# First feed-forward products of seven rounds: weights standing, high and low x moving side by side, hidden layer not transposed

## The chip, the cores and the metric

The kernel runs on one core of a Trainium2 chip. The metric is the device time of one execution in microseconds (us); lower is better. Engines: TensorE (PE in the rows; its weight loads are PEld), VectorE (DVE), ScalarE (ACT), GpSimd (POOL) and the sync engine (SP), whose queue issues the loads.

## What is computed

The reference is two transformer blocks one after the other, on 256 tokens of width 2048, in float32. The change touches the feed-forward part of the first block:

```
def sq_relu_mlp(h, w1, w2):
    return jnp.square(jax.nn.relu(h @ w1)) @ w2
x = x + gm * sq_relu_mlp(modulate(x, norm_mlp_w[l], sm, cm), w_ff1[l], w_ff2[l])
```

w_ff1 is 2048 x 8192, w_ff2 is 8192 x 2048. `gm`, `sm` and `cm` are conditions, products of a vector with columns of w_mod.

## The kernel before

Every large product is made from split operands: a float32 weight tile is loaded (`raw`, four slots of 1 MB), ScalarE rounds it to fp32r (`whi`, line 591), VectorE takes the difference (`wlo`, line 1085), each in two halves, and TensorE adds three products: high x times high weight, low x times high weight, high x times low weight. A **unit** is one 1 MB load: 512 rows of the weight by 512 columns, `whi` and `wlo` hold two units each. The semaphore `units_used` counts halves that TensorE is done with; ScalarE may round unit u's half once TensorE is done with the same half of unit u-2. The loads are issued by SP in one fixed order (line 394), load n once load n-4 has been used up.

`multiply` (line 1867) makes the products of a unit: for each pair of k-tiles and each of the two blocks of 128 tokens it loads x as the standing operand (128 x 128) and moves 512 weight columns through, 24 matmuls in all (line 1887). The result is in rows of tokens.

The feed-forward phase (`mlp`) is eight **rounds** of 16 units, e = 0 to 7 (`quarter` in each engine's program). In a round, units 0 to 7 are the first product for 1024 hidden columns, in two groups of four units, each into two PSUM banks. ScalarE takes a group with relu into `hid` (line 857), VectorE squares it (line 1528). The second product needs the hidden layer with its columns on the partitions, so TensorE transposes it (`turn_rows`, line 1968) in 8 pairs of 128-column blocks per token block, that is 16 transposes a round, in runs of 4, 4 and 8; ScalarE rounds each run of four out of PSUM into `hhi` (line 609) and VectorE takes the difference into `hlo` (line 1106). Units 8 to 15 are the second product, four groups of two units, each added into `yacc` (line 1565).

Round 0 begins with its own order (`first_columns`), in which the transposes of the normed x are spread. In rounds 0 to 3 four more loads a round, slices of w_mod, stand in the same four slots behind units 4, 6, 11 and 13 (`CONDITIONS_MLP`), and VectorE sums each with a column of the condition vector (`sum_rows`, lines 1255 and 1257); such a slot is released by `cond_summed`. In round 7 VectorE also adds four finished conditions (`add_condition`, line 1408), which wait for TensorE's sums (line 2153), and TensorE transposes rows for the next phase.

Elsewhere two places have weights standing and x moving, 256 columns at a time: the z gates of both attention phases (`multiply_gate`, line 2308) and the narrow unit of gate columns (line 2478), whose load has rows of 512 B (line 459).

Of the kernel before, what the change touches and what calls it, by code (L numbers as in the profile page):

```python
# [51 lines left out]
          ("mlp", 128, 48), ("a_in", 20, 5), ("a_z", 16, 4), ("a_out", 16, 4), ("b_att", 29, 8), ("b_z", 16, 4),  # L52
# [41 lines left out]
for _u in range(UNITS):  # L94
# [7 lines left out]
          ("a", 8), ("b", 8)]  # L102
BUILD = {}
# [34 lines left out]

def plus(base, step, i):

    return base if i is None else base + step * i


def dit_kernel(nc, a, out):
# [9 lines left out]
    xhi = sb("xhi", [P, KT, L], F32R)  # L154
    xlo = sb("xlo", [P, KT, L], F32R)
# [76 lines left out]
    hid = v3(rows[:, 0:2048], W1)  # L232
# [144 lines left out]
    def _(sp):  # L377
        count = {"load": 0, "plain": 0, "mod": 0, "sum": 0}

        def load(kind, src, narrow=False):  # L380
# [12 lines left out]
            to = raw[:, n % 4].rearrange("p k (c n) -> p (k c) n", n=P) if narrow else raw[:, n % 4]  # L393
            sp.dma_start(to, src.rearrange("(k p) n -> p k n", p=P)).then_inc(raw_in[n % 4], 16)
# [12 lines left out]
        def load_unit(src, narrow=False):  # L407
            u = count["plain"]
            load("plain", src, narrow)
# [49 lines left out]
        load_unit(a["b_w_in"][:, D + 6 * KVG * HD:D + 6 * KVG * HD + P], narrow=True)  # L459
# [114 lines left out]
    def _(act):  # L574
# [279 lines left out]
        def quarter(e, u0, b0, loads=16):  # L854
            def relu(n):
                group_done(u0 + 4 * n + 3, e, 16)
                act.activation(hid[:, :, n * NW:(n + 1) * NW], banks(n), ACT.Relu).then_inc(acc_freed, 1)

            def hidden(g):
                build(b0 + g, 2 * g, hhi, i=e, per=4)  # L860

            split(u0 + 3, 3, e, 16, loads)
            relu(0)
            split(u0 + 6, 2, e, 16, loads)
            hidden(0)
            split(u0 + 8, 1, e, 16, loads)
            hidden(1)
            split(u0 + 9, 1, e, 16, loads)
            relu(1)
            hidden(2)  # L870
            hidden(3)
            for n in range(4):
# [21 lines left out]
        with act.Fori(0, 4) as e:  # L894
            quarter(e, UNIT["mlp"], BUILD["hidden"], loads=20)
# [177 lines left out]
    def _(dve):  # L1073
# [443 lines left out]
        def quarter(e, u0, g0, b0, s0, last=False, conditions=False):  # L1517
            def split_with_condition(u, k):

                for half in range(2):  # L1520
                    split_halves(2 * u + half, 1, e, 16)
                    if conditions:
                        sum_rows(cond_sum[:, bass.ds(e * NW, NW)], SUM["mlp"] + k, k, (2 * half, 2 * half + 1), e)

            def square(n):
                dve.wait_ge(acc_freed, plus(g0 + n + 1, 6, e))
# [3 lines left out]
            def hidden(g):  # L1530
                build(b0 + g, 2 * g, hhi, hlo, i=e, per=4)

            split(u0 + 3, 2, e, 16)
            split_with_condition(u0 + 5, 0)
            square(0)
            if last:
                add_condition(4)
                add_condition(5)
            split(u0 + 6, 1, e, 16)
            split_with_condition(u0 + 7, 1)  # L1540
            hidden(0)
            split(u0 + 8, 1, e, 16)
            hidden(1)
            split(u0 + 9, 1, e, 16)
# [3 lines left out]
            if last:  # L1548
                add_condition(6)
                add_condition(7)  # L1550
            for n in range(4):
                if n in (1, 2):
                    split_with_condition(u0 + 10 + 2 * n, n + 1)
# [7 lines left out]
                cols = slice(n * NW, (n + 1) * NW)  # L1561
                part = yacc[:, :, cols]
                if n == 0:
                    dve.wait_ge(zeroed, 1)
                dve.tensor_tensor(part, banks(n), part, ALU.add).then_inc(acc_freed, 1)
                if last:
                    dve.wait_ge(modcol_taken, 1 + CONDITIONS1 + 8)
                    dve.wait_ge(acc_freed, g0 + 2 + n + 1)
# [14 lines left out]
        with dve.Fori(0, 4) as e:  # L1583
            end = looped(12, 4)
            quarter(e, UNIT["mlp"], GROUP["mlp"], BUILD["hidden"], 0, conditions=True)
# [277 lines left out]
    def _(pe):  # L1863
# [29 lines left out]


# [325 lines left out]
        def quarter(e, u0, g0, b0, s0, first=False, last=False):  # L2220
            def hidden(pairs):
                turn_rows(b0, hid, pairs, i=e, per=4,
                          ready=lambda g: pe.wait_ge(squared, plus(s0 + g // 2 + 1, 2, e)))

            if first:
                first_columns()
            else:
                product(u0, 0, 4, built=built("mlp"), i=e, per=16, g_count=g0, g_per=6)

            pe.wait_ge(acc_freed, plus(g0, 6, e))  # L2230
            for k in range(4):
                multiply(u0 + 4 + k, k, 4, 2, i=e, per=16)
                if last and k in (0, 3):
                    for b in (4, 5) if k == 0 else (6, 7):
                        sum_rows(b)
# [3 lines left out]
            pe.wait_ge(acc_freed, plus(g0 + 1, 6, e))  # L2239
            for tiles in ((0, 1, 2), (3,)):  # L2240
                multiply(u0 + 8, 0, 2, 0, 0, hhi, hlo, e, 16, tiles=tiles, rounded=plus(b0 + 2, 4, e) if tiles[0] == 0 else None)
                if tiles[0] == 0:
                    hidden((2, 3))
            multiply(u0 + 9, 1, 2, 0, 0, hhi, hlo, e, 16, rounded=plus(b0 + 4, 4, e))
            for n in range(1, 4):
                pe.wait_ge(acc_freed, plus(g0 + 1 + n, 6, e))
# [368 lines left out]
```

## Time and profile before

| | |
|---|---|
| median of 3 runs | 2292.61 us (2292.25 to 2293.01) |
| profiled execution: time, span | 2292.78 us, 2291.0 us |
| TensorE, busy share of the span | 99% |
| VectorE, ScalarE, GpSimd | 68%, 46%, 3% |
| share of the chain that ended last: TensorE | 95% |
| mean DMA rate | 207 GB/s |

The time of an execution is a little above the span of its trace. Busy time of matmuls is pipelined: two that follow each other overlap in the rows, so the cost of one is read from the distance between two starts. "Idle before" is the time an engine stood before the instructions of a row, with what released it.

### The profile page before, as it was taken

How to read it: one execution, taken by the hardware profiler on the slowest of the kernel's cores; microseconds unless marked ns; L12 is line 12 of the kernel's file. 1: busy time of each engine (PE TensorE's matmuls, PEld its weight loads, DVE VectorE, ACT ScalarE, POOL GpSimd, SP SyncE). 2: the span in 40 equal slices, each digit the busy share in tenths (PEclk: the TensorE clock that was granted, in tenths of full speed). 3: DMA queues.
4: the chain of work that ended last, by engine and by line, in shares of the span. 5: the costliest groups of instructions: out<-in, count | busy, mean ns of one | idle time of the engine just before them, and what ended most of it. 6: DMA issues, size and time to landing. Idle time of an engine off the chain costs nothing.

```text
span 2291.0 us, 30464 instructions
## 1 busy us (share of the span) xinstructions
PE 2258.2 (99%) x11867; PEld 1853.3 (81%) x11867; DVE 1552.7 (68%) x2299; ACT 1064.8 (46%) x1589; POOL 72.4 (3%) x91
## 2 busy tenths in 40 slices
PE   6999999999999999999999999999999999999998
PEld 3777787877888788888888888888988888899977
DVE  2577798777888776676655555764686545578865
ACT  4343234555543644344444443454555454466644
POOL 1000001110000100000000000000000000000000
PEclk8999999999999999999999999999999999999999
DMA  9989884444689677667656555555444576432243
GB/s 369 334 307 316 299 301 160 146 144 152 222 299 322 211 272 242 223 235 248 229 188 196 183 186 185 180 184 184 157 126 141 184 231 211 157 120 93 93 133 125
DMA packets 235011, 474.61 MB, mean 207 GB/s; under 512 B 7784, under 2 KB 10176, under 8 KB 233872
## 3 DMA queue, kind: packets, MB, share of 16 engines
q1 hardware_dynamic: 231280, 460.35, 59.7%
q0 software_dynamic: 3296, 12.53, 1.6%
q8 instruction: 79, 1.29, 0.2%
q14 instruction: 36, 0.29, 0.0%
q10 hardware_dynamic: 320, 0.13, 0.0%
HBM read 470.89 MB, written 2.10 MB: 206 GB/s over the span
## 4 chain that ended last, share of the span: by engine, by line
PE 95%; DVE 2%; DMA 2%; ACT 1%; issue 1%; SPq 0%; POOLq 0%; POOL 0%; DVEq 0%
PE acc L1887 74%; PE acc L2308 8%; PE acc L2350 2%; PE aux L2384 2%; PE turn L2364 2%; PE aux L1920 1%; PE turn L1968 1%; DMA raw<-in_w_o 1%; DVE wlo L1085 1%; DMA arena<-in_x 1%; PE turn L2105 1%; PE acc L2120 1%; PE turn L2263 0%; PE acc L2090 0%; PE aux L2408 0%
## 5 line engine op out<-in xcount | busy, mean ns | idle before, releaser
L1085 DVE TENSOR_TENSOR wlo<-raw,whi 128x1024 fp32r<-128x1024 f32 x674 | 819.9, 1224 | 550.8 <-ACT whi L591 545.3
L591 ACT ACTIVATE whi<-raw 128x1024 fp32r<-128x1024 f32 x674 | 710.7, 1059 | 975.1 <-PE acc L1887 851.3
L1887 PE MATMUL acc<-whi,xhi 128*128 128x512 f32 x1536 | 424.4, 398 | 4.4 <-ACT xhi L673 2.6
L1887 PE MATMUL acc<-whi,xlo 128*128 128x512 f32 x1536 | 413.0, 390 | 0.5 <-DVE xlo L1485 0.5
L1887 PE MATMUL acc<-wlo,xhi 128*128 128x512 f32 x1536 | 412.7, 390 | 0.0
L1887 PEld LDWEIGHTS acc<-whi,xhi 128*128 128x128 f32 x1536 | 281.2, 188 | 85.8 <-issue 24.9
L1887 PEld LDWEIGHTS acc<-whi,xlo 128*128 128x128 f32 x1536 | 288.6, 188 | 62.7 <-DVE xlo L1485 1.0
L1887 PEld LDWEIGHTS acc<-wlo,xhi 128*128 128x128 f32 x1536 | 288.9, 188 | 61.2
L1887 PE MATMUL acc<-whi,hhi 128*128 128x512 f32 x512 | 139.7, 392 | 0.0
L1887 PE MATMUL acc<-whi,hlo 128*128 128x512 f32 x512 | 138.2, 389 | 0.0
L1887 PE MATMUL acc<-wlo,hhi 128*128 128x512 f32 x512 | 138.2, 389 | 0.0
L1887 PEld LDWEIGHTS acc<-whi,hlo 128*128 128x128 f32 x512 | 96.1, 188 | 20.1
L1887 PEld LDWEIGHTS acc<-wlo,hhi 128*128 128x128 f32 x512 | 96.1, 188 | 20.1
L1887 PEld LDWEIGHTS acc<-whi,hhi 128*128 128x128 f32 x512 | 95.3, 188 | 19.5 <-issue 0.5
L1887 PE MATMUL acc<-whi,ghi 128*128 128x512 f32 x384 | 107.0, 397 | 0.5 <-ACT whi L591 0.5
L1887 PE MATMUL acc<-whi,glo 128*128 128x512 f32 x384 | 104.1, 390 | 0.0
L950 ACT ACTIVATE arena<-arena,m 128x128 f32<-128x128 f32 (+3 forms) x192 | 85.1, 445 | 40.8 <-DVE m L1669 40.8
L1887 PE MATMUL acc<-wlo,ghi 128*128 128x512 f32 x384 | 104.0, 389 | 0.0
L1257 DVE SCALAR_TENSOR_TENSOR arena<-raw,cflat,arena 128x512 f32<-128x512 f32 x120 | 90.0, 750 | 3.5
L1257 DVE SCALAR_TENSOR_TENSOR qkv<-raw,cflat,qkv 128x512 f32<-128x512 f32 (+1 forms) x120 | 89.9, 749 | 2.3
L2308 PE MATMUL acc<-xhi,whi 128*128 128x256 f32 x512 | 86.0, 290 | 0.0
L1887 PEld LDWEIGHTS acc<-whi,glo 128*128 128x128 f32 x384 | 72.1, 188 | 15.3
(329 smaller groups left out, 2329.7 us busy)
## 6 DMA issues: line engine op xcount, KB each, us to landing
raw<-in_w_ff SPq DMA_DIRECT2D x128, 1024.0 KB, 5.2
raw<-in_w_mod SPq DMA_DIRECT2D x96, 1024.0 KB, 7.3
raw<-in_w_in SPq DMA_DIRECT2D x64, 1024.0 KB, 5.3
raw<-in_b_w_in SPq DMA_DIRECT2D x45, 1024.0 KB, 5.0
raw<-in_a_w_in SPq DMA_DIRECT2D x36, 1024.0 KB, 5.1
raw<-in_w_o SPq DMA_DIRECT2D x16, 1024.0 KB, 7.1
raw<-in_a_w_out SPq DMA_DIRECT2D x16, 1024.0 KB, 5.2
raw<-in_b_w_out SPq DMA_DIRECT2D x16, 1024.0 KB, 5.0
```

The costliest lines, as they stand in the source:

```text
L591: act.activation(whi[:, k % 2, on], raw[:, n % 4, on], ACT.Copy).then_inc(hi_ready, 1)
L950: ins = act.activation(x, x, ACT.Exp, scale=-1.0, bias=m8[:, q % 2, k:k + 1], accum_out=s8[:, q % 2, k:k + 1])
L1085: dve.tensor_tensor(wlo[:, k % 2, on], raw[:, LOAD_OF_UNIT[k] % 4, on], whi[:, k % 2, on].bitcast(F32), ALU.subtract)\
L1257: ins = dve.scalar_tensor_tensor(total, raw[:, n % 4, kk], x, total, ALU.mult, ALU.add)
L1887: mm = pe.matmul(acc[:, bank0 + t, :], x[:, tile(kt), t * P:(t + 1) * P], w[:, u % 2, kk], start=kt == k_first and x is hi and w is whi, s ...
L1920: mm = pe.matmul(bank[32 * kk:32 * (kk + 1), :], cflat[:, 2 * kt:2 * kt + 32], raw[:, n % 4, kk], start=k == 0, stop=k == 3, tile_position ...
L1968: mm = pe.transpose(turn[:, n % 2, k * L + t * P:k * L + (t + 1) * P], src[:, t, (2 * g + k) * P:(2 * g + k + 1) * P], ident[:, :])
L2105: mm = pe.matmul(turn[:, c, :], slabT[on, t * P:(t + 1) * P], slabT[on, 256:768], start=True, stop=True)
L2308: mm = pe.matmul(acc[:, 2 + c // 2, c % 2 * L:(c % 2 + 1) * L], w[:, c * P:(c + 1) * P], x[:, kt, :], start=kt == 0 and c % 2 == 0 and w i ...
L2350: mm = pe.matmul(acc[:, c, u * keys:(u + 1) * keys], at["qT"][on, g, t, j, :], at["kT"][u][on, g * L:g * L + keys], start=True, stop=True)
L2364: mm = pe.transpose(turn[:, c, o:o + P], prob[:, c, u, k * P:(k + 1) * P], ident[:, :])
L2384: mm = pe.matmul(aux[c * HD:(c + 1) * HD, n % 2, to:to + w], at["v"](g, u, k), pT[:, 512 * c + o:512 * c + o + w], start=i == k == u == 0, ...
```

## The change

In rounds 1 to 7 the first product is made by a new function, `multiply_turned`. Its unit is 1024 rows of w_ff1 by 256 columns (8 k-tiles, two column blocks; the load has rows of 1 KB in place of 2 KB). 128 x 128 blocks of weights are the standing operand. x moves: `xhi` and `xlo` are now the two halves of one tile `x2`, and 512 columns, 256 of high and 256 of low x, go through the high weights into the two halves of a PSUM bank; then 256 columns of high x go through the low weights into the first half. There are four groups of two units. The result has the hidden columns on the partitions. VectorE adds the two halves (`tensor_reduce`), then makes relu and square in one instruction; ScalarE rounds into `hhi` from SBUF, VectorE takes the difference into `hlo`. The transposes of the hidden layer and ScalarE's relu are gone from these rounds. The sums of conditions stand behind the difference of groups 1 and 2 in place of between the halves of units 5 and 7; in round 7 the additions of conditions stand behind groups 1 and 3. Round 0 keeps its form (`first_quarter`). The second product is as before, but for the hidden tiles that its first two units wait for.

```diff
 PHASES = [("front", 32, 48), ("att", 32, 8), ("up", 16, 8), ("wo", 16, 4),
-          ("mlp", 128, 48), ("a_in", 20, 5), ("a_z", 16, 4), ("a_out", 16, 4), ("b_att", 29, 8), ("b_z", 16, 4),
+          ("mlp", 128, 62), ("a_in", 20, 5), ("a_z", 16, 4), ("a_out", 16, 4), ("b_att", 29, 8), ("b_z", 16, 4),
           ("b_out", 16, 4)]
...
 
 BUILDS = [("front", 16), ("mix", 8), ("mlp", 8), ("hidden", 32),
           ("a", 8), ("b", 8)]
+BUILT_TURNED = 28
...
          12: ("turn", "b_ks"), 13: ("norm", 1), 14: ("turn", "b_kw"), 15: ("turn", "b_q2")}
 
 
+def turned_of(g):
...
     wlo = sb("wlo", [P, 2, UK, NW], F32R)
-    xhi = sb("xhi", [P, KT, L], F32R)
-    xlo = sb("xlo", [P, KT, L], F32R)
+    x2 = sb("x2", [P, 2, KT, L], F32R)
+    xhi, xlo = x2[:, 0], x2[:, 1]
+
+    narrow_hi, narrow_lo = (w[:, :, :, :].rearrange("p s k (c n) -> p s (k c) n", n=L) for w in (whi, wlo))
...
-    hid = v3(rows[:, 0:2048], W1)
+    hid, hid4 = v3(rows[:, 0:2048], W1), v3(rows[:, 0:2048], NW)
...
                     sp.wait_ge(cond_summed, before.count("sum"))
-            to = raw[:, n % 4].rearrange("p k (c n) -> p (k c) n", n=P) if narrow else raw[:, n % 4]
...
         for e in range(8):
-            for n in range(2):
-                for k in range(4):
-                    load_unit(a["w_ff1"][k * 512:(k + 1) * 512, e * W1 + n * NW:e * W1 + (n + 1) * NW])
+            if e == 0:
+                column_blocks(a["w_ff1"], 2)
+            else:
+                for n in range(4):
+                    for k in range(2):
+                        load_unit(a["w_ff1"][k * W1:(k + 1) * W1, e * W1 + n * L:e * W1 + (n + 1) * L], width=L)
             for n in range(4):
                 for k in range(2):
...
-            act.wait_ge(turned, plus(g + 1, per, i))
+            act.wait_ge(turned, plus(turned_of(g), per, i))
...
+        def first_quarter():
+            u0, b0 = UNIT["mlp"], BUILD["hidden"]
+
...
+            split(u0 + 10, 9)
+
+        def quarter(e, u0, b0, loads=16):
+            for g in range(4):
+                split(u0 + 3 + 2 * g, 1, e, 16, loads)
+                act.wait_ge(squared, plus(b0 - BUILD["hidden"] - 4 + 2 + g + 1, 4, e))
+                act.activation(hhi[:, 2 * g:2 * g + 2, :], v3(hid4[:, g], L), ACT.Copy).then_inc(hi_rounded, 1)
+                if g < 3:
+                    split(u0 + 4 + 2 * g, 1, e, 16, loads)
             for n in range(4):
                 split(u0 + 10 + 2 * n, 1, e, 16, loads)
                 if e is None and n:
...
-        with act.Fori(0, 4) as e:
-            quarter(e, UNIT["mlp"], BUILD["hidden"], loads=20)
+        first_quarter()
+        with act.Fori(0, 3) as e:
+            quarter(e, UNIT["mlp"] + 16, BUILD["hidden"] + 4, loads=20)
         with act.Fori(0, 3) as e:
             quarter(e, UNIT["mlp"] + 4 * 16, BUILD["hidden"] + 4 * 4)
...
+        def quarter(e, u0, g0, b0, last=False, conditions=False):
+            def split_and_sum_some(u, k):
+
+                if conditions:
+                    split_with_condition(u, k, cond_sum[:, NW:4 * NW][:, bass.ds(e * NW, NW)], SUM["mlp"] + 4, e)
+                else:
+                    split(u, 1, e, 16)
+
+            for g in range(4):
+                u = u0 + 2 * g + 3
+                part = v3(hid4[:, g], L)
+                split_halves(2 * u, 1, e, 16)
+                group_done(u - 2, e, 16)
+                dve.tensor_reduce(part, banks(g).rearrange("p b (c n) -> p b n c", c=2), AX.X, ALU.add).then_inc(acc_freed, 1)
+                dve.wait_ge(acc_freed, plus(g0 + g + 1, 8, e))
+                dve.scalar_tensor_tensor(part, part, 0.0, part, ALU.max, ALU.mult).then_inc(squared, 1)
+                split_halves(2 * u + 1, 1, e, 16)
+                dve.wait_ge(hi_rounded, plus(b0 + g + 1, 4, e))
+                dve.tensor_tensor(hlo[:, 2 * g:2 * g + 2, :], part, hhi[:, 2 * g:2 * g + 2, :].bitcast(F32), ALU.subtract)\
+                   .then_inc(xt_ready, 1)
+                if conditions and g in (1, 2):
+                    sum_rows(cond_sum[:, NW:4 * NW][:, bass.ds(e * NW, NW)], SUM["mlp"] + 4 + g - 1, g - 1, range(UK), e)
+                if last and g in (1, 3):
+                    add_condition(3 + g)
+                    add_condition(4 + g)
+                if g < 3:
+                    split(u + 1, 1, e, 16)
+            for n in range(4):
+                if n in (1, 2):
+                    split_and_sum_some(u0 + 10 + 2 * n, n + 1)
                 else:
                     split(u0 + 10 + 2 * n, 1, e, 16)
                 if last and n:
...
                 if last:
+                    cols = slice(n * NW, (n + 1) * NW)
+                    part = yacc[:, :, cols]
                     dve.wait_ge(modcol_taken, 1 + CONDITIONS1 + 8)
-                    dve.wait_ge(acc_freed, g0 + 2 + n + 1)
+                    dve.wait_ge(acc_freed, g0 + 4 + n + 1)
                     link(dve.tensor_tensor(part, part, bc(gm_b[:, cols].unsqueeze(1), [P, T, NW]), ALU.mult))
...
+        first_quarter()
+        with dve.Fori(0, 3) as e:
+            end = looped(12, 3)
+            quarter(e, UNIT["mlp"] + 16, GROUP["mlp"] + 6, BUILD["hidden"] + 4, conditions=True)
             end()
         with dve.Fori(0, 3) as e:
-            quarter(e, UNIT["mlp"] + 4 * 16, GROUP["mlp"] + 4 * 6, BUILD["hidden"] + 4 * 4, 8)
-        quarter(None, UNIT["mlp"] + 7 * 16, GROUP["mlp"] + 7 * 6, BUILD["hidden"] + 7 * 4, 14, last=True)
+            quarter(e, UNIT["mlp"] + 4 * 16, GROUP["mlp"] + 30, BUILD["hidden"] + 4 * 4)
+        quarter(None, UNIT["mlp"] + 7 * 16, GROUP["mlp"] + 54, BUILD["hidden"] + 7 * 4, last=True)
...
+
+        def multiply_turned(u, k, bank0, parts=range(2), i=None, per=0):
+
+            for part in parts:
+                pe.wait_ge(hi_ready, plus(2 * u + 1 + part, 2 * per, i))
+                tiles = [(kk, 8 * k + kk, c) for kk in range(4 * part, 4 * part + 4) for c in range(2)]
+                for kk, kt, c in tiles:
+                    pe.matmul(v3(acc[:, bank0 + c, :], L), narrow_hi[:, u % 2, kk, c * P:(c + 1) * P], x2[:, :, kt, :],
+                              start=kt == 0, stop=False, skip_group_check=True)
+                pe.wait_ge(lo_ready, plus(2 * u + 1 + part, 2 * per, i))
+                for kk, kt, c in tiles:
+                    mm = pe.matmul(acc[:, bank0 + c, 0:L], narrow_lo[:, u % 2, kk, c * P:(c + 1) * P], xhi[:, kt, :],
+                                   start=False, stop=kt == KT - 1, skip_group_check=True)
+                mm.then_inc(units_used, 1)
 
...
+        def quarter(e, u0, g0, b0, last=False):
+            for g in range(4):
+                pe.wait_ge(acc_freed, plus(g0 + g - 1, 8, e))
+                for k in range(2):
+                    multiply_turned(u0 + 2 * g + k, k, 2 * (g % 2), i=e, per=16)
+                    if last and k == 0 and g in (2, 3):
+                        for b in (4, 5) if g == 2 else (6, 7):
+                            sum_rows(b)
+
+            for n in range(4):
+                pe.wait_ge(acc_freed, plus(g0 + 3 + n, 8, e))
                 for k in range(2):
                     for tiles in ((0, 1), (2, 3)):
-                        multiply(u0 + 8 + 2 * n + k, k, 2, 2 * (n % 2), 0, hhi, hlo, e, 16, tiles=tiles)
-                        if last and k == 1 and tiles[0] == 0:
+                        built_of = b0 + 2 * k + (2 if k == 0 else 1 + tiles[0] // 2)
+                        multiply(u0 + 8 + 2 * n + k, k, 2, 2 * (n % 2), 0, hhi, hlo, e, 16, tiles=tiles,
+                                 rounded=plus(built_of, 4, e) if n == 0 else None)
+                        if last and n and k == 1 and tiles[0] == 0:
                             turn_rows("a", res3, (2 * n - 2, 2 * n - 1), ready=lambda g: pe.wait_ge(res_done, g // 2 + 1))
 
-        quarter(None, u0, g0, BUILD["hidden"], 0, first=True)
-        with pe.Fori(1, 7) as e:
-            quarter(e, u0, g0, BUILD["hidden"], 0)
-        quarter(None, u0 + 7 * 16, g0 + 7 * 6, BUILD["hidden"] + 7 * 4, 14, last=True)
+        first_quarter()
+        with pe.Fori(0, 6) as e:
+            quarter(e, u0 + 16, g0 + 6, BUILD["hidden"] + 4)
+        quarter(None, u0 + 7 * 16, g0 + 54, BUILD["hidden"] + 7 * 4, last=True)
```

## Rows read from the trace of the kernel before

**Rows 1.** The page: the chain by engine and line, clock, a weight load.
```profile
PEclk8999999999999999999999999999999999999999
...
PE 95%; DVE 2%; DMA 2%; ACT 1%; issue 1%; SPq 0%; POOLq 0%; POOL 0%; DVEq 0%
...
L1887 PEld LDWEIGHTS acc<-whi,xhi 128*128 128x128 f32 x1536 | 281.2, 188 | 85.8 <-issue 24.9
```

**Rows 2.** Windows: us; PE, PEld, DVE, ACT, POOL busy; clock; DMA share; GB/s.
```profile
907.00:996.00 89.00, 89.00 (x402) 73.76 (x401) 59.39 (x59) 37.53 (x38) 0.00 (x0) 1.00 0.69 237
1262.00:1351.00 89.00, 89.00 (x402) 73.76 (x401) 48.44 (x42) 37.69 (x39) 0.00 (x0) 1.00 0.58 189
```

**Rows 3.** The chain through one round: start us, us, what.
```profile
1001.52 0.87 PE turn L1968 x8
1002.39 72.10 PE acc L1887 x318
1074.49 0.44 PE turn L1968 x4
...
1080.41 0.44 PE turn L1968 x4
...
1090.42 0.87 PE turn L1968 x8
```

**Rows 4.** Timeline of TensorE around four transposes: start us, us, what.
```profile
1074.33 0.60 PE L1968 MATMUL turn<-ident,arena 128*128 128x128 f32 x4
...
1077.52 1.07 PE L1887 MATMUL acc<-whi,xhi 128*128 128x512 f32 x4
1078.43 1.07 PE L1887 MATMUL acc<-whi,xlo 128*128 128x512 f32 x4
1079.34 1.07 PE L1887 MATMUL acc<-wlo,xhi 128*128 128x512 f32 x4
```

**Rows 5.** Timeline of TensorE in the z gates and the narrow unit.
```profile
1621.45 0.64 PE L2308 MATMUL acc<-xlo,whi 128*128 128x256 f32 x4
1621.93 0.64 PE L2308 MATMUL acc<-xhi,wlo 128*128 128x256 f32 x4
...
1900.84 0.28 PE L2478 MATMUL acc<-xlo,whi 128*128 128x256 f32 x1
1900.96 1.09 PE L1887 MATMUL acc<-whi,xhi 128*128 128x512 f32 x4
```

**Rows 6.** Groups by line and shape: busy us, mean ns, idle before.
```profile
L857 ACT ACTIVATE arena<-acc 128x1024 f32<-128x1024 f32 x16 | 16.1, 1009 | 0.0
L609 ACT ACTIVATE hhi<-turn 128x512 fp32r<-128x512 f32 x32 | 18.0, 588 | 22.1 <-PE turn L1968 22.1
L751 ACT ACTIVATE xhi<-arena 128x512 fp32r<-128x512 f32 x8 | 4.5, 624 | 0.1
...
L1106 DVE TENSOR_TENSOR hlo<-turn,hhi 128x512 fp32r<-128x512 f32 x32 | 21.3, 686 | 15.8 <-ACT hhi L609 15.3
L1337 DVE TENSOR_REDUCE lam<-turn 128x2 f32<-128x1024 f32 x16 | 19.6, 1225 | 10.2 <-PE turn L2105 9.8
L1528 DVE TENSOR_TENSOR arena<-arena 128x1024 f32<-128x1024 f32 x16 | 19.5, 1220 | 0.5
L1257 DVE SCALAR_TENSOR_TENSOR qkv<-raw,cflat,qkv 128x512 f32 x60 | 45.0, 749 | 1.1
```

**Rows 7.** Loads of 512 B rows, of 2 KB rows, longest landing; one load waited on.
```profile
raw<-in_b_w_in SPq DMA_DIRECT2D x1, 1024.0 KB, 5.8
...
raw<-in_b_w_in SPq DMA_DIRECT2D x1, 1024.0 KB, 5.0
...
DMA to landing us min/median/max: 4.8/5.2/8.7
...
1067.44 4.36 SPq L394 DMA_DIRECT2D raw<-in_w_ff  x3
...
1073.11 1.06 ACT L591 ACTIVATE whi<-raw 128x1024 fp32r<-128x1024 f32 x1 [2.97 <-DMA raw<-in_w_ff]
```

More of the change, by code:

```diff
@@ L378, in _, with load @@
         count = {"load": 0, "plain": 0, "mod": 0, "sum": 0}
-        def load(kind, src, narrow=False):
+        def load(kind, src, width=NW):
             n = count["load"]
@@ L405, in load_summed, with load_unit @@
             load("sum", a["w_mod"][k * 512:(k + 1) * 512, c0:c0 + NW])
-        def load_unit(src, narrow=False):
+        def load_unit(src, width=NW):
             u = count["plain"]
-            load("plain", src, narrow)
+            load("plain", src, width)
             for kind in LOADED_BEHIND[u]:
@@ L852, in _ @@
                 split_halves(u0 + g, 1)
-        def quarter(e, u0, b0, loads=16):
+        def first_quarter():
+            u0, b0 = UNIT["mlp"], BUILD["hidden"]
             def relu(n):
-                group_done(u0 + 4 * n + 3, e, 16)
+                group_done(u0 + 4 * n + 3)
                 act.activation(hid[:, :, n * NW:(n + 1) * NW], banks(n), ACT.Relu).then_inc(acc_freed, 1)
             def hidden(g):
-                build(b0 + g, 2 * g, hhi, i=e, per=4)
-            split(u0 + 3, 3, e, 16, loads)
+                build(b0 + g, 2 * g, hhi)
+            split(u0 + 3, 3)
             relu(0)
-            split(u0 + 6, 2, e, 16, loads)
+            split(u0 + 6, 2)
             hidden(0)
-            split(u0 + 8, 1, e, 16, loads)
+            split(u0 + 8, 1)
             hidden(1)
-            split(u0 + 9, 1, e, 16, loads)
+            split(u0 + 9, 1)
             relu(1)
@@ L1514, in _, with add_hidden, split_with_condition, first_quarter @@
         norm_b = lambda k: cols2[:, V_NORM_B + k:V_NORM_B + k + 1]
[L1517 to L1523, printed above, removed]
+        def add_hidden(n):
+            cols = slice(n * NW, (n + 1) * NW)
+            part = yacc[:, :, cols]
+            if n == 0:
+                dve.wait_ge(zeroed, 1)
+            dve.tensor_tensor(part, banks(n), part, ALU.add).then_inc(acc_freed, 1)
+        def split_with_condition(u, k, total, c0, e=None):
+            for half in range(2):
+                split_halves(2 * u + half, 1, e, 16)
+                sum_rows(total, c0 + k, k, (2 * half, 2 * half + 1), e)
+        def first_quarter():
+            u0, g0, b0 = UNIT["mlp"], GROUP["mlp"], BUILD["hidden"]
+            total, c0 = cond_sum[:, 0:NW], SUM["mlp"]
             def square(n):
-                dve.wait_ge(acc_freed, plus(g0 + n + 1, 6, e))
+                dve.wait_ge(acc_freed, g0 + n + 1)
                 part = hid[:, :, n * NW:(n + 1) * NW]
@@ L1530, in hidden @@
             def hidden(g):
-                build(b0 + g, 2 * g, hhi, hlo, i=e, per=4)
-            split(u0 + 3, 2, e, 16)
-            split_with_condition(u0 + 5, 0)
+                build(b0 + g, 2 * g, hhi, hlo)
+            split(u0 + 3, 2)
+            split_with_condition(u0 + 5, 0, total, c0)
             square(0)
[L1536 to L1540, printed above, removed]
+            split(u0 + 6, 1)
+            split_with_condition(u0 + 7, 1, total, c0)
             hidden(0)
-            split(u0 + 8, 1, e, 16)
+            split(u0 + 8, 1)
             hidden(1)
-            split(u0 + 9, 1, e, 16)
+            split(u0 + 9, 1)
             square(1)
@@ L2218, in first_columns, with first_quarter @@
                         turn_pair(7)
-        def quarter(e, u0, g0, b0, s0, first=False, last=False):
+        def first_quarter():
             def hidden(pairs):
[L2222 to L2230, printed above, removed]
+                turn_rows("hidden", hid, pairs, ready=lambda g: pe.wait_ge(squared, g // 2 + 1))
+            b0 = BUILD["hidden"]
+            first_columns()
+            pe.wait_ge(acc_freed, g0)
@@ L2231, in quarter @@
             for k in range(4):
[L2232 to L2235, printed above, removed]
+                multiply(u0 + 4 + k, k, 4, 2)
                 if k in (1, 2):
                     hidden((k - 1,))
-            pe.wait_ge(acc_freed, plus(g0 + 1, 6, e))
+            pe.wait_ge(acc_freed, g0 + 1)
             for tiles in ((0, 1, 2), (3,)):
-                multiply(u0 + 8, 0, 2, 0, 0, hhi, hlo, e, 16, tiles=tiles, rounded=plus(b0 + 2, 4, e) if tiles[0] == 0 else None)
+                multiply(u0 + 8, 0, 2, 0, 0, hhi, hlo, tiles=tiles, rounded=b0 + 2 if tiles[0] == 0 else None)
@@ L2242, in quarter @@
                 if tiles[0] == 0:
                     hidden((2, 3))
-            multiply(u0 + 9, 1, 2, 0, 0, hhi, hlo, e, 16, rounded=plus(b0 + 4, 4, e))
+            multiply(u0 + 9, 1, 2, 0, 0, hhi, hlo, rounded=b0 + 4)
             for n in range(1, 4):
-                pe.wait_ge(acc_freed, plus(g0 + 1 + n, 6, e))
+                pe.wait_ge(acc_freed, g0 + 1 + n)
+                for k in range(2):
+                    multiply(u0 + 8 + 2 * n + k, k, 2, 2 * (n % 2), 0, hhi, hlo)
+        def quarter(e, u0, g0, b0, last=False):
+            for g in range(4):
+                pe.wait_ge(acc_freed, plus(g0 + g - 1, 8, e))
+                for k in range(2):
+                    multiply_turned(u0 + 2 * g + k, k, 2 * (g % 2), i=e, per=16)
[4 more added lines that the diff above has]
+                pe.wait_ge(acc_freed, plus(g0 + 3 + n, 8, e))
```

26 lines of the change are left out of this document (13 added, 13 removed).

## The prediction

> **What bounds the kernel now.** I read the page first: busy shares, the chain that ended last, the TensorE clock [rows 1]. TensorE is busy 99% of the span, its clock is full outside the edges, and the chain is 95% TensorE. So only what shortens or lengthens TensorE's own queue, or makes it wait, can move the time. Then the windows of one round with conditions and one without, each 89 us long [rows 2]: TensorE is busy all through, VectorE 59.4 us in the first and 48.4 us in the second, ScalarE 37.5 and 37.7 us, DMA 69% and 58%. The other engines have room. Then the chain within one round [rows 3]: it is TensorE alone, matmuls of line 1887 broken by the transposes of line 1968 (4, 4 and 8). The group of 8 starts at 1001.52 and again at 1090.42, so a round takes 88.90 us. Last, the matmuls one by one [rows 4]: four of 512 columns start each 0.907 us (1077.52, 1078.43, 1079.34), 226.7 ns each. 384 of them are 87.04 us; the 16 transposes, with the slower starts behind them, cost the other 1.86 us.
>
> The profiled execution took 2292.78 us, 1.8 us above its span of 2291.0; the median of the runs is 2292.61, so 0.2 us less. The sum below is made against 2292.78.
>
> **The change, part by part.** It touches rounds 1 to 7 of the feed-forward phase; round 0 keeps its form.
>
> *Columns moved.* A unit was 24 matmuls of 512 columns. Now it is, for each of 8 k-tiles and 2 column blocks, one matmul of 512 columns (high and low x side by side against the high weights) and one of 256 (high x against the low weights): 16 and 16. The columns are the same, 12,288, but there are 32 matmuls instead of 24. What a 256-column one costs is in the rows of the z gates, which have weights standing and x moving: four start each 0.48 us, 120.0 ns each, in an unbroken row of units [rows 5]. It is so too where high and low weights alternate and where a 512 follows a 256 (1900.84 to 1900.96) [rows 5]. Both widths pay their columns (213.3 and 106.7 ns at 2.4 GHz) plus 13.3 ns. A weight load is shown as 188 ns [rows 1], longer than the 120.0 ns between two starts, so loads overlap and their cost is inside the 120.0. The unit becomes 16 x 226.7 + 16 x 120.0 = 5.547 us in place of 5.440: +0.107 us, +0.85 us in the 8 units of a round.
>
> The Trainium skill ("TensorE: Matmul & The Clock Gate", Back-to-back issue gap) gives N/2.4 + 2.5 ns per matmul. By it the 64 extra matmuls of a round would cost 0.16 us, not 0.85, and the whole change would come to 2280.7. The rows of this case speak against it at both widths.
>
> *Transposes.* All 16 of a round go: -1.86 us. Their place on TensorE is taken by nothing; the hidden columns come out of PSUM already turned.
>
> *The two segments.* The moving operand of the 512-column matmul lies in two pieces of 256 columns, in two halves of one tile. No row shows a moving operand in pieces. Lower bound: nothing more than a 512 in one piece, 226.7 ns. Upper bound: as two matmuls of 256, 240.0 ns, which is 13.3 ns more on 16 x 8 x 7 = 896 matmuls, 11.9 us. I take the lower: a cost of a second instruction has no second instruction here to carry it.
>
> *ScalarE.* Out: two relus (1.01 us each) and four roundings from PSUM (0.59). In: four roundings of the same size from SBUF (0.62, as line 751) [rows 6]. It gets 2.0 us lighter. Its new wait, on the square, stands behind the rounding of unit 2g+3 and ahead of that of unit 2g+4, which TensorE wants 11.1 us after group g ends; the square is there 2.1 us after it. Hidden.
>
> *VectorE.* Out: two squares of 1024 (1.22) and four differences from PSUM (0.69), 5.2 us. In, four times: a reduction of 1024 PSUM elements to 512 (1.23, as line 1337, the nearest; twice that as upper bound, since it reads the halves a stride apart; nothing excludes a little less, but it sets no end), relu and square in one (0.75, as line 1257), a difference (0.69): 10.7 us [rows 6]. So +5.5 us of a 87.9 us round, on 59.4. Within one group of two units (11.09 us) VectorE has four splits at a pitch of 1.15, 4.6 us, and these 2.7 us: 7.3. In rounds 1 to 3 groups 1 and 2 also carry a sum of conditions, 3.0 us: 10.3 of 11.09. Hidden, but with less than 1 us of room; if the reduction cost 2.4 us, these two groups would take 11.5 and VectorE would be the bound there.
>
> *Ready at the second product.* Group 3 ends, TensorE turns to unit 8 and wants its hidden tiles 8.2 us later (unit 8 and half of unit 9). Reduction, square, half a split, rounding and difference are done 4 us after the end of the group. Hidden.
>
> *Loads.* The units of w_ff1 come as 1 KB rows, 1024 packets instead of 512. The same queue's one load of 512 B rows landed in 5.8 us where its neighbours took 5.0 [rows 7]; so I add 0.3 us, between nothing and 0.8. The order of loads stays, but one release moves: unit 7's load waits for the condition behind unit 4 to be summed, and the sum now stands behind group 1's reduction, square, split and difference. With T the end of unit 3: 1.3 + 0.8 + 1.2 + 0.7 + 2.9 = T + 6.9, where it was T + 4.0 before (issue at 1067.44, the round began at 1041.68, unit 3 ended at 1063.4). The load then took 5.7 us (ScalarE rounds at 1073.11, waiting on it for 2.97) [rows 7]; it is the first of a pair and there is nothing ahead of it. Now: T + 6.9 + 6.0 = 12.9; rounded 14.0; split 15.3; only then does VectorE come to group 2's reduction (whose products ended at T + 11.1), square, second half, difference, sum (3.1) and the first half of unit 8: 1.3 + 0.8 + 1.2 + 0.7 + 3.1 + 1.2 = 8.3, T + 23.6. TensorE wants that half of the low weights at T + 22.2 + 1.8 = 24.0. It holds, by 0.4 us. This is the one tight place, in three rounds.
>
> *Last round.* The additions of conditions 4 and 5 stand behind group 1's difference and wait for TensorE's two sums behind unit 4, about T + 6.5. Queued behind them is the split of unit 6, done at about T + 10.3 and wanted at T + 12.9. Hidden.
>
> **Sum.** Per round -1.86 + 0.85 = -1.01; seven rounds -7.1 us. 2292.78 - 7.1 = 2285.7 for an execution like the profiled one, 2285.5 beside the median. That is -0.31%. A measurement of this kernel tells some 0.2% (4.6 us) from no change.
>
> **Rivals.**
> - *Load and sum run late in rounds 1 to 3.* For it: the room of 0.4 us above, and a longest landing in these rounds of 8.7 us where I take 6.0 [rows 7]. Every us beyond the room is one that TensorE stands, three times over. At 7.5 us: 1.1 x 3 = +3.3, 2288.8; at 8.7: 2.3 x 3 = +6.9, 2292.4. A reduction of 2.4 us costs about the same: 1.2 in each of two groups less the room, some 1.6 per round, 2290.3. Against it: the longest landing is that of a load with others ahead of it, and VectorE's reduction in line 1337 costs what every 1024-element operation there does. 14% together.
> - *Slower: the two pieces.* Every 512-column matmul of the new form pays a second 13.3 ns at the seam: -7.1 + 11.9 = +4.8, so 2292.6 + 4.8 = 2297.4. It turns the sign from 7.9 ns a matmul on (7.1 us over 896). For it: no row excludes it. Against it: the 13.3 ns come once per instruction at both widths, whatever its columns. 9%.
> - *The extra matmuls are nearly free.* If the 13.3 ns hung on something other than the count of matmuls (the way the z gates take their operands, say), the unit would cost no more than before, and only the transposes would count: 2292.6 - 13.0 = 2279.6; the skill's rule above ends near it. Against it: 256 columns cost 120.0 in two different orders of operands, and 512 carry the same 13.3. 5%.
> - *The change does not do what it says.* If the transposes were covered by other waits their loss would bring nothing: but the chain runs through them and TensorE has no idle time around them [rows 3, 4]. 2%, at +6.0, 2298.6.
>
> **How the numbers follow.** Forecast 70%, at 2285.5, with its own range 2283.5 to 2287.5. The late load spreads from 2287 to 2292. I go down to 2282.0, towards the cheap side, and up to 2290.5, which takes in most of the late loads and the slow reduction; the pieces, the void change and the cheapest case stay out, 16 to 18% in all. Faster by over 0.2% (under 2288.0): 70% + 5% + a quarter of the late loads, 0.78. Same: the rest of these, 0.11. Slower: the pieces and the void change, 0.11.
>
> **What would show it.** In the changed profile: no transposes on TensorE between rounds; a 512 start each 226.7 ns and a 256 each 120.0 in rounds 1 to 7, eight of the one and eight of the other; a round of 87.9 us; VectorE up by 5.5 us a round and never named before a TensorE idle. The forecast is wrong if 512-column starts lie 240 ns apart (pieces), if TensorE stands before unit 7 or 8 in rounds 1 to 3 (load, sum, or a reduction far over 1.23 us), or if ScalarE or VectorE stands between the end of a group and the first hidden tile.

## Result and profile after

The changed kernel takes **2296.15 us** (median of 22 runs, 2294.0 to 2298.28) against 2292.17 us before (22 runs, 2291.39 to 2294.75): ratio 1.0016, 95% interval 1.001 to 1.0022. It is slower by 4.0 us. The forecast was 2285.5 us and faster.

The profiled execution has a span of 2294.5 us. First the page of the changed kernel, the lines that answer to [rows 1]: clock, chain, and the new form's groups (busy us, mean ns, idle before, releaser).

```profile
PEclk8999999999999999999999999999999999999999
...
PE 93%; DVE 3%; DMA 2%; issue 1%; ACT 1%; SPq 0%; DVEq 0%; POOLq 0%; POOL 0%; ACTq 0%
...
L1964 PE MATMUL acc<-x,whi 128*128 128x512 f32 x896 | 225.3, 393 | 2.5 <-ACT whi L602 2.5
...
L1968 PE MATMUL acc<-x,wlo 128*128 128x256 f32 x896 | 124.9, 282 | 0.0
...
raw<-in_w_ff SPq DMA_DIRECT2D x128, 1024.0 KB, 5.7
```

The clock is as before. TensorE's share of the chain fell from 95 to 93%; VectorE has 3 where it had 2, and TensorE now shows idle time before line 1964, released by ScalarE's rounding. Where it lies comes out of the chain in order of time (start us, us, what), of which these are the long runs of second products of rounds 2 to 5:

```profile
1003.95 42.04 PE acc L1950 x184
...
1095.16 42.02 PE acc L1950 x184
1181.84 43.55 PE acc L1950 x192
1270.06 43.55 PE acc L1950 x192
```

The last two are a round without conditions: 1270.06 - 1181.84 = **88.22 us**, 0.68 less than the 88.90 before [rows 3]. The first two are one with conditions: 91.21 us, 2.31 more than before. From the first matmul of each round in the trace, rounds 1 to 3 take 91.31, 90.94 and 91.19 us, rounds 4 to 6 take 88.21 each. So the change gains 0.69 us in each of seven rounds (-4.8, with round 7, which was not timed by itself, counted as the others) and loses 8.8 us in three: 3.1 + 2.7 + 3.0. The two together are +4.0, the measured difference.

The same chain inside a round with conditions says what the 3 us are:

```profile
1065.52 1.84 PE acc L1964 x8
1067.36 0.97 PE acc L1968 x8
1068.35 1.23 DVE arena L1601
...
1071.35 0.68 DVE hlo L1606
...
1074.04 0.76 DVE qkv L1280
1074.82 9.89 DMA raw<-in_w_ff
1084.82 1.06 ACT whi L602
...
1087.05 1.23 DVE arena L1601
...
1090.05 0.68 DVE hlo L1606
1091.43 0.76 DVE qkv L1280
```

The reader is to see a loop that leaves TensorE: the group of unit 3 ends at 1068.3, VectorE reduces it, takes the difference and sums the condition; at 1074.82 that releases unit 7's load, which takes 9.89 us; ScalarE rounds it, VectorE splits it and only then reduces the next group, and comes to unit 8 last. TensorE's own timeline shows the two places where it stands (idle before, releaser):

```profile
1082.11 2.00 PE L1964 MATMUL acc<-x,whi 128*128 128x512 f32 x8
...
1085.93 2.12 PE L1964 MATMUL acc<-x,whi 128*128 128x512 f32 x8 [0.86 <-ACT whi L602]
...
1092.56 1.07 PE L1950 MATMUL acc<-whi,hlo 128*128 128x512 f32 x4
1095.16 1.19 PE L1950 MATMUL acc<-wlo,hhi 128*128 128x512 f32 x4 [1.53 <-DVE wlo L1108]
```

By the distances of the starts, unit 7 comes 1.0 us late (1085.93, where eight 512s and eight 256s from 1082.11 end at 1084.90) and unit 8's low weights 1.7 us (1095.16, where 1092.56 and four matmuls make 1093.47). Behind each stand the next starts lose another 0.1 us; together that is the round's 3.0 us. The windows of a round with and one without conditions, as [rows 2] (us; PE, PEld, DVE, ACT, POOL busy; clock; DMA share; GB/s):

```profile
954.00:1042.00 88.00, 85.89 (x437) 72.91 (x436) 62.55 (x64) 34.66 (x35) 0.00 (x0) 1.00 0.66 227
1225.00:1313.00 88.00, 88.00 (x449) 75.18 (x448) 53.27 (x49) 36.50 (x36) 0.00 (x0) 1.00 0.60 190
```

VectorE is at 62.6 of 88 us where TensorE stands, so it is not its load that binds, but its order. Its and ScalarE's new instructions cost what the nearest rows had promised [rows 6]:

```profile
L1601 DVE TENSOR_REDUCE arena<-acc 128x512 f32<-128x1024 f32 x28 | 34.2, 1223 | 10.2 <-PE acc L1968 10.2
L1603 DVE SCALAR_TENSOR_TENSOR arena<-arena 128x512 f32<-128x512 f32 x28 | 19.4, 692 | 1.0
L1606 DVE TENSOR_TENSOR hlo<-arena,hhi 128x512 fp32r<-128x512 f32 x28 | 19.2, 684 | 0.0
...
L891 ACT ACTIVATE hhi<-arena 128x512 fp32r<-128x512 f32 x28 | 17.7, 633 | 44.4 <-DVE arena L1603 44.4
```

### The profile page after: what moved, and what is told of

Same layout as the page of the kernel before. It is cut to its first block, busy times and chain, and to the rows that moved or that the text cites. A ratio compares the mean times of both kernels' runs of the same rounds, so it can differ in the third digit from the quotient of the medians.

```text
span 2294.5 us, 31062 instructions
## 1 busy us (share of the span) xinstructions
PE 2255.5 (98%) x12203; PEld 1865.0 (81%) x12203; DVE 1586.6 (69%) x2341; ACT 1055.0 (46%) x1575; POOL 72.4 (3%) x91
## 4 chain that ended last, share of the span: by engine, by line
PE 93%; DVE 3%; DMA 2%; issue 1%; ACT 1%; SPq 0%; DVEq 0%; POOLq 0%; POOL 0%; ACTq 0%
PE acc L1950 62%; PE acc L2394 8%; PE acc L1964 7%; PE acc L1968 4%; PE acc L2436 2%; PE aux L2470 2%; PE turn L2450 2%; DMA raw<-in_w_ff 1%; PE aux L1997 1%; DMA arena<-in_x 1%; PE turn L2182 1%; DVE wlo L1108 1%; DVE qkv L1280 1%; PE turn L2045 1%; PE acc L2197 1%
## 5 line engine op out<-in xcount | busy, mean ns | idle before, releaser
L1950 PE MATMUL acc<-whi,x 128*128 128x512 f32 x2176 | 551.3, 395 | 4.9 <-ACT x L684 2.6
L1950 PEld LDWEIGHTS acc<-whi,x 128*128 128x128 f32 x2176 | 402.6, 188 | 113.9 <-issue 24.7
L1950 PE MATMUL acc<-wlo,x 128*128 128x512 f32 x1088 | 292.9, 390 | 0.0
L1950 PEld LDWEIGHTS acc<-wlo,x 128*128 128x128 f32 x1088 | 204.8, 188 | 43.6
L1964 PE MATMUL acc<-x,whi 128*128 128x512 f32 x896 | 225.3, 393 | 2.5 <-ACT whi L602 2.5
L1964 PEld LDWEIGHTS acc<-x,whi 128*128 128x128 f32 x896 | 161.7, 189 | 33.2 <-ACT whi L602 3.5
L2394 PE MATMUL acc<-x,whi 128*128 128x256 f32 x1024 | 147.2, 286 | 0.0
L2394 PEld LDWEIGHTS acc<-x,whi 128*128 128x128 f32 x1024 | 131.4, 191 | 0.6
L1968 PEld LDWEIGHTS acc<-x,wlo 128*128 128x128 f32 x896 | 122.2, 190 | 8.8
L1968 PE MATMUL acc<-x,wlo 128*128 128x256 f32 x896 | 124.9, 282 | 0.0
```

What stands on the lines that cost most here:

```text
L1950: mm = pe.matmul(acc[:, bank0 + t, :], x[:, tile(kt), t * P:(t + 1) * P], w[:, u % 2, kk], start=kt == k_first and x is hi and w is whi, s ...
L1964: pe.matmul(v3(acc[:, bank0 + c, :], L), narrow_hi[:, u % 2, kk, c * P:(c + 1) * P], x2[:, :, kt, :], start=kt == 0, stop=False, skip_grou ...
L1968: mm = pe.matmul(acc[:, bank0 + c, 0:L], narrow_lo[:, u % 2, kk, c * P:(c + 1) * P], xhi[:, kt, :], start=False, stop=kt == KT - 1, skip_g ...
L2394: mm = pe.matmul(acc[:, 2 + c // 2, c % 2 * L:(c % 2 + 1) * L], w[:, c * P:(c + 1) * P], x[:, kt, :], start=kt == 0 and c % 2 == 0 and w i ...
```

## Experiments

**The late load.** Three kernels each take away one condition of it. The first changes only the rows of the load:

```diff
-                for n in range(4):
-                    for k in range(2):
-                        load_unit(a["w_ff1"][k * W1:(k + 1) * W1, e * W1 + n * L:e * W1 + (n + 1) * L], width=L)
+                for n in range(2):
+                    for k in range(4):
+                        load_unit(a["w_ff1"][k * 512:(k + 1) * 512, e * W1 + n * NW:e * W1 + (n + 1) * NW])
```

> The changed kernel, but w_ff1 of rounds 1 to 7 is loaded as 512 rows by 512 columns, in rows of 2 KB as before the change (so these units multiply other weights than the reference's; the work on every engine is the same). In the changed kernel a round without conditions takes 88.21 us and one with conditions 91.31, 90.94 and 91.19: TensorE stands 0.8 to 1.2 us before unit 7 and 1.7 us in unit 8, behind unit 7's load, which lands 9.6 to 10.0 us after its issue (the last of its 16 parts; the 15th is there at 6.1 to 7.4). Theory A (rows of 1 KB make this load late when other loads stand behind it): unit 7 lands in 5.7 to 6.5 us, rounds 1 to 3 come to 88.2 to 88.7 us, and the time falls by 7.5 to 9 us, to about 2287.5. Theory B (the later release alone does it, three loads go out within 2.5 us and share the engines whatever their rows): the landing stays above 8.5 us and the time within 2 us of 2296.

Measured: 2288.18 us, ratio to the kernel before 0.998 (0.9971 to 0.9989), 8.0 us under the changed kernel. All rounds 1 to 6 take 88.21 us.

The second moves VectorE's sum ahead of its wait for the group:

```diff
                 split_halves(2 * u, 1, e, 16)
+                if conditions and g in (1, 2):
+                    sum_rows(cond_sum[:, NW:4 * NW][:, bass.ds(e * NW, NW)], SUM["mlp"] + 4 + g - 1, g - 1, range(UK), e)
                 group_done(u - 2, e, 16)
...
-                if conditions and g in (1, 2):
-                    sum_rows(cond_sum[:, NW:4 * NW][:, bass.ds(e * NW, NW)], SUM["mlp"] + 4 + g - 1, g - 1, range(UK), e)
```

> The changed kernel, but VectorE sums the conditions of groups 1 and 2 ahead of its wait for the group, where it was idle, and not behind the difference. Unit 7's load then goes out about 4 us sooner. Both theories of the late load expect the stalls to go, since even a landing of 10 us is in time then: rounds 1 to 3 at 88.2 us each, the time 8.5 to 9 us below the changed kernel, 2287.3, 4.8 below the kernel before. A third theory, that VectorE has too much to do in these groups wherever the sum stands, expects a stall of 1 us or more per round to stay, in unit 8.

Measured: **2287.39 us**, ratio 0.9978 (0.9969 to 0.9987), 8.8 us under the changed kernel and 4.8 under the one before. It leaves nothing of the computation out. Its chain in rounds 1 to 3, the same runs as above:

```profile
908.58 43.55 PE acc L1950 x192
...
996.80 43.55 PE acc L1950 x192
...
1085.01 43.55 PE acc L1950 x192
```

The distance is 88.21 us, and 192 matmuls of the second product stand unbroken where the changed kernel had 184. VectorE's timeline shows what the move does:

```profile
1062.66 2.33 DVE L1280 SCALAR_TENSOR_TENSOR qkv<-raw,cflat,qkv 128x512 f32 x3
1065.02 1.22 DVE L1603 TENSOR_REDUCE arena<-acc 128x512 f32<-128x1024 f32 x1
```

The sum begins at 1062.14, 0.5 us before TensorE ends unit 3 (at 1062.7; units here are 5.58 us long), and ends as the load of unit 7 goes out, at 1065.02: 2.3 us after the group's end, where it had been 6.5. So most of the sum doesn't fill idle time. It stands ahead of the reduction, square, split and difference, which need not be done before the load. The reduction starts 2.3 us later than it could, and nobody misses it. The third theory (too much work wherever the sum stands) is gone.

The third holds the followers back:

```diff
+            if kind == "plain" and count["plain"] - 1 in [UNIT["mlp"] + 16 * e + 8 for e in (1, 2, 3)]:
+                sp.wait_ge(raw_in[(n - 1) % 4], 16 * ((n - 1) // 4 + 1))
```

> The changed kernel, but in rounds 1 to 3 SP issues the load of unit 8 only when unit 7's has landed. Theory A and B both say that the loads behind it hold unit 7's last part back: it lands in 5.2 to 5.5 us, as single loads of 1 KB rows do in this kernel (5.5 at 1070.82 of the raw trace), and the stall before unit 7 goes; that in unit 8 falls by the same, so the time falls by 6 to 9 us. If unit 7's load is late for its own sake (its place in memory, an instruction fetch), it stays near 10 us and the time near 2296.

Measured: 2287.9 us, ratio 0.9981 (0.9972 to 0.9991), rounds of 88.21 us. Unit 7's load goes out no sooner after its group than in the changed kernel (6.5 us), but it isn't late: neither its place in memory nor its short rows alone make it so.

The fourth brings the rows of 1 KB into rounds 1 to 7 of the kernel before:

```diff
-            for n in range(2):
-                for k in range(4):
-                    load_unit(a["w_ff1"][k * 512:(k + 1) * 512, e * W1 + n * NW:e * W1 + (n + 1) * NW])
+            for n in range(4):
+                for k in range(2):
+                    if e:
+                        load_unit(a["w_ff1"][k * W1:(k + 1) * W1, e * W1 + n * L:e * W1 + (n + 1) * L], narrow=L)
```

> The kernel before, but w_ff1 of rounds 1 to 7 is loaded as 1024 rows by 256 columns in rows of 1 KB, as in the changed kernel (other weights than the reference's in these units; same work). Theory A: unit 7's load, with unit 8's right behind it, lands 1 to 4 us later than the 5.7 us of the kernel before, but its room there is some 4 us, so the time moves by less than 2 us (0 to +2). Theory B: no change in landing or time (within 0.5 us).

Measured: 2293.43 us, ratio 1.0003 (0.9994 to 1.0012): 1.2 us more in the medians, which can't be told from no change. The landings decide. The line of unit 7's load in round 3, with the us from issue to landing, stands below for each kernel; first the changed one, then with rows of 2 KB (e1), sums early (e2), followers held (e3), and the kernel before with rows of 1 KB (e4).

```profile
raw<-in_w_ff SPq DMA_DIRECT2D x1, 1024.0 KB, 9.9
```
```profile
raw<-in_w_ff SPq DMA_DIRECT2D x1, 1024.0 KB, 5.4
```
```profile
raw<-in_w_ff SPq DMA_DIRECT2D x1, 1024.0 KB, 5.2
```
```profile
raw<-in_w_ff SPq DMA_DIRECT2D x1, 1024.0 KB, 5.3
```
```profile
raw<-in_w_ff SPq DMA_DIRECT2D x1, 1024.0 KB, 9.8
```

| load of unit 7 | other loads within 2.5 us behind it | landing |
|---|---|---|
| 1 KB rows (changed) | two | 9.6 to 10.0 us |
| 2 KB rows (e1) | two | 5.4 to 5.5 |
| 1 KB rows (e2, e3) | none | 5.2 to 5.5 |
| 1 KB rows in the kernel before (e4) | one at 0.4, one at 4 us | 8.7 to 9.8 |

It takes both: short rows, and loads queued behind. A load signals in 16 parts. In the changed kernel's landing events 15 parts of unit 7's load are there 6.1 to 7.4 us after the issue in rounds 1 to 3, and one comes 2.2 to 3.8 us after the others. The two loads behind are in rows of 2 KB (w_ff2), and the packets of the same trace show what becomes of the last part. Here are the packets of 1081 to 1084, and the queue's share from 1086 to 1089:

```profile
DMA packets 580, 1.15 MB, mean 383 GB/s; under 512 B 15, under 2 KB 24, under 8 KB 580
```
```profile
q1 hardware_dynamic: 41, 0.08, 6.9%
```

In the first stretch only nine packets of 1 KB are left (24 less 15 of 4 B). They run one after another and took 154 to 512 ns each, while the packets of 2 KB around them took 84 (median). With nothing behind the load (e3) its packets of 1 KB took 46 from 4 us after the issue to the last. In the second stretch the queue's share is about that of one engine in sixteen: it works off what the others have long done. So the late part is one engine's, whose packets of 1 KB were held up while the others moved rows of 2 KB. In rounds 1 and 2 the slowest such packets took 494 and 211 ns.

The kernel before had room for a late part: in e4 ScalarE waits for this load, and TensorE stands 0.4 us in one of three rounds (idle before).

```profile
1076.69 2.01 ACT L595 ACTIVATE whi<-raw 128x1024 fp32r<-128x1024 f32 x2 [7.22 <-DMA raw<-in_w_ff]
```
```profile
1086.99 1.20 PE L1891 MATMUL acc<-whi,hlo 128*128 128x512 f32 x4 [0.42 <-DVE hlo L1110]
```

So the later release isn't needed for the late landing, only for TensorE to feel it. Neither half of the change is slow by itself: rows of 1 KB with the old order cost 1.2 us in the medians (the interval goes from -1.4 to +2.8), the new order with rows of 2 KB leaves the rounds at 88.21. Together they cost 8 to 9.

**The gain per round.** Forecast -1.01 us, measured -0.69. The changed kernel in a round without conditions:

```profile
1233.58 2.00 PE L1964 MATMUL acc<-x,whi 128*128 128x512 f32 x8
1235.42 1.11 PE L1968 MATMUL acc<-x,wlo 128*128 128x256 f32 x8
1236.37 2.00 PE L1964 MATMUL acc<-x,whi 128*128 128x512 f32 x8
```

Eight of 512 and eight of 256 start over 2.79 us (1233.58 to 1236.37), where 8 x (226.7 + 120.0) ns are 2.774; 16 times a round that is 0.3 us. One by one the starts behind a run of 256s are 233, 236, 228, 232, 231, then 227 ns apart, and the first 256s behind a 512 are 114 and 119. Three kernels, all with the sums early, ask where this comes from. Alternating:

```diff
                 pe.wait_ge(hi_ready, plus(2 * u + 1 + part, 2 * per, i))
                 tiles = [(kk, 8 * k + kk, c) for kk in range(4 * part, 4 * part + 4) for c in range(2)]
+                pe.wait_ge(lo_ready, plus(2 * u + 1 + part, 2 * per, i))
                 for kk, kt, c in tiles:
                     pe.matmul(v3(acc[:, bank0 + c, :], L), narrow_hi[:, u % 2, kk, c * P:(c + 1) * P], x2[:, :, kt, :],
                               start=kt == 0, stop=False, skip_group_check=True)
-                pe.wait_ge(lo_ready, plus(2 * u + 1 + part, 2 * per, i))
-                for kk, kt, c in tiles:
                     mm = pe.matmul(acc[:, bank0 + c, 0:L], narrow_lo[:, u % 2, kk, c * P:(c + 1) * P], xhi[:, kt, :],
                                    start=False, stop=kt == KT - 1, skip_group_check=True)
```

> The changed kernel with the sums early (as e2_sum_early), and in a unit each matmul of 512 columns is followed at once by its matmul of 256, in place of eight and eight. In e2 a round takes 88.21 us where 128 x (226.7 + 120.0) ns and 43.52 us make 87.90; the 0.31 us lie in the first five 512s behind each run of 256s (233, 236, 228, 232, 231 ns). Theory S (each change from 256 to 512 costs some 20 ns once): 128 changes a round in place of 16, the round grows by up to 2.2 us, to 90.4. Theory P (the weight load of the next matmul is not hidden behind a short one and is caught up behind long ones, so only runs of short ones cost): the round comes down to 87.9 to 88.0 us and the time falls by 1.5 to 2 us below e2.

Measured: 2291.27 us, ratio 0.9996 (0.9987 to 1.0005); a round takes 88.79 us.

```profile
1174.77 43.58 PE acc L1950 x192
1263.57 43.58 PE acc L1950 x192
```

Neither theory: a pair costs 353.6 ns on average, 7 more than 346.7, so 128 changes cost 0.89 us where 16 cost 0.31. A return to 512 costs 20 ns behind a run of 256s (27 in the five slow starts, less 7 in the first two 256s) and 7 when single. Theory P, under which alternating should have gained, is wrong; theory S has the sign right and the size wrong.

All sixteen 512s of a unit first, then the 256s:

```diff
+            tiles = lambda part: [(kk, 8 * k + kk, c) for kk in range(4 * part, 4 * part + 4) for c in range(2)]
             for part in parts:
                 pe.wait_ge(hi_ready, plus(2 * u + 1 + part, 2 * per, i))
-                tiles = [(kk, 8 * k + kk, c) for kk in range(4 * part, 4 * part + 4) for c in range(2)]
-                for kk, kt, c in tiles:
+                for kk, kt, c in tiles(part):
...
+            for part in parts:
                 pe.wait_ge(lo_ready, plus(2 * u + 1 + part, 2 * per, i))
-                for kk, kt, c in tiles:
+                for kk, kt, c in tiles(part):
```

> As e2_sum_early, but TensorE makes all sixteen 512s of a unit and then all sixteen 256s, so it goes from 256 to 512 once a unit in place of twice. Theory S and P alike: 8 of the 16 changes of a round go, the round comes to 88.05 us, the time to 1 us below e2 (2286.3), unless the later release of the first half of the weights makes TensorE wait (then idle time before a unit appears and the round is longer than 88.21).

Measured: **2286.29 us**, ratio 0.9971 (0.996 to 0.9982), the lowest of the versions that leave nothing out; a round takes 88.05 us, as expected. A unit starts each 5.56 us:

```profile
1227.67 3.82 PE L1964 MATMUL acc<-x,whi 128*128 128x512 f32 x16
1231.32 2.08 PE L1969 MATMUL acc<-x,wlo 128*128 128x256 f32 x16
1233.23 3.82 PE L1964 MATMUL acc<-x,whi 128*128 128x512 f32 x16
```

One piece in place of two:

```diff
-                    pe.matmul(v3(acc[:, bank0 + c, :], L), narrow_hi[:, u % 2, kk, c * P:(c + 1) * P], x2[:, :, kt, :],
+                    pe.matmul(v3(acc[:, bank0 + c, :], L), narrow_hi[:, u % 2, kk, c * P:(c + 1) * P], x2[:, 0, kt - kt % 2:kt - kt % 2 + 2, :],
```

> As e2_sum_early, but the 512 moving columns are two neighbouring k-tiles of high x, in one piece (so the low x is left out and the product is another). If the two pieces cost anything, the 512s fall below their 226 to 236 ns and the round comes to 87.9; if the extra lies in the change of width alone, the starts and the round of 88.21 us stay as they are, within 0.05 us.

Measured: 2286.91 us, ratio 0.9976 (0.9967 to 0.9986), the round 88.21 us, the starts the same as in e2. Two pieces cost nothing.

**The transposes.** The last run prices the term that was to bring the gain, in the kernel before:

```diff
-        def turn_rows(name, src, pairs=range(8), i=None, per=0, ready=None):
+        def turn_rows(name, src, pairs=range(8), i=None, per=0, ready=None, blocks=range(2)):
...
-                for k in range(2):
-                    for t in range(T):
+                for k in blocks:
+                    for t in blocks:
...
-                turn_rows(b0, hid, pairs, i=e, per=4,
+                turn_rows(b0, hid, pairs, i=e, per=4, blocks=range(1),
```

> The kernel before with 1 in place of 4 transposes in each run of four of the hidden layer (three quarters of it are not transposed and the second product takes old values; relu, square, rounding and difference stay). It prices the transposes: 96 fewer in eight rounds. If their price is what the rows say (16 with the restart behind them 1.86 us, four alone 0.44), the round falls from 88.90 to between 87.4 and 87.7 us and the time by 9.5 to 12 us. If the restart behind a run is most of it, the fall is under 6 us.

Measured: 2282.91 us, ratio 0.9958 (0.9942 to 0.9973), 9.4 us less, just under the 9.5 to 12 expected; from its chain a round takes 87.62 us:

```profile
1071.02 0.11 PE turn L1968
...
1086.28 0.22 PE turn L1968 x2
1086.50 72.14 PE acc L1887 x318
1158.64 0.11 PE turn L1968
```

Twelve transposes less are 1.28 us (88.90 - 87.62), 107 ns each; the four that are left stand at 0.11 each. With these four the sixteen are 1.7 of the 1.86 us that I had booked. The rest, 0.1 to 0.2 us, is still there in e6 (87.62 less 87.04 of matmuls and 0.44 of transposes): the slower starts behind the three runs. The term stands.

## Why the prediction was wrong

- **Bound and cover.** Right: TensorE's queue is the time, and where nothing is late the round length times seven gives the change. e2 shows it without the stalls: 2287.4, and 2292.2 - 7 x 0.69 = 2287.4.
- **Transposes, -1.86 a round.** Right (e6, within 0.1 to 0.2 us).
- **Columns moved, +0.85 a round.** Mis-sized: 88.21 - 88.90 + 1.86 = +1.17. The 226.7 and 120.0 ns hold inside a run of one width, but every return from 256 to 512 costs 20 ns net. My row of the switch (1900.84 to 1900.96) showed only the distance up to the first 512 and not the ones behind it: 1900.96 opens a group of four in 0.93 us, to be had from that same timeline, where 0.907 is the pace. 0.31 us x 7 = 2.2 us. The Trainium skill's N/2.4 + 2.5 ns ("TensorE: Matmul & The Clock Gate", Back-to-back issue gap), which that section gives for a matmul taken alone, isn't met in this stream: e7's sixteen 256s start over 1.91 us (1231.32 to 1233.23), 119 ns each, not 109.
- **The two segments.** Taken at nothing, measured at nothing (e8). The rival that turned on them ends on the measured side, but for a reason that isn't there.
- **ScalarE, VectorE, the hidden tiles, the last round.** Right: 1.22 us for the reduction, no wait on any of them but through the load. VectorE's square costs 0.69, not 0.75.
- **Loads.** The step that failed. It followed the right chain to the right place: release at T + 6.9 (measured T + 6.5), room 0.4 us, "every us beyond the room is one that TensorE stands, three times over". The failed sentence is "so I add 0.3 us", with "it is the first of a pair". It went by one load of 512 B rows that nothing stood behind [rows 7], and by a load of 2 KB rows that had followers; neither row had both. Nor was it a pair: the later release puts three loads within 2.5 us (1074.82, 1075.2, 1077.3). Unit 7's load landed 9.6 to 10.0 us after its issue in place of 6.0. That is 3.6 to 4.0 us, less the 0.4 by which it went out sooner than forecast and the room of 0.4: 2.8 to 3.2 a round, measured 2.7 to 3.1. So the rest of this chain was right. The first rival named this mechanism, priced it at 2292.4 for a landing of 8.7 us, and was given 14% together with another. A release moved into a chain with 0.4 us of room deserved more than that, and a range that took in its far end. The two terms together are the miss: 2285.5 + 2.2 (columns) + 8.8 (load) = 2296.5, measured 2296.15.

The Trainium skill ("DMA: Bandwidth & Descriptors", Specifications) puts the smallest transfer for full rate at 512 B. That speaks of rate, and for a load with nothing close behind it size of row matters little here too: unit 7's took 5.2 to 5.8 us in rows of 1 KB and 5.1 to 5.6 in rows of 2 KB. For the landing of a load with others behind it, it's no guide: 9.6 to 10.0 us in rows of 1 KB, 5.4 to 5.5 in rows of 2 KB.

What stays open: why it is one engine of the sixteen that falls behind, and what holds its packets of 1 KB up while others move rows of 2 KB. That was not tried.

## What to carry to other kernels

When a change moves work behind a group's last product, list what that work releases. A slot of a load ring that came free 4.2 us later cost nothing (e1 against e2) until the load itself took longer. The cure was not less work but its order: work that frees a slot goes ahead of work that nobody waits for yet. A landing time measured on a quiet queue is no bound for the same load with others right behind it.

## What was not expected of the hardware

A load of 1 MB in rows of 1 KB, with two loads in rows of 2 KB issued within 2.5 us behind it, had 15 of its 16 parts in 6.1 to 7.4 us and the last at 9.6 to 10.0; with none that close it took 5.2 to 5.8, and in rows of 2 KB with the same followers 5.4 to 5.5. Its last packets took up to 512 ns each in place of 46. And matmuls of 512 columns behind a run of 256s start 233, 236, 228, 232 and 231 ns apart before they return to 226.7; strict alternation costs 7 ns a pair, two pieces of moving operand cost nothing.
